# Cached-page attention as one stream beside projection and recurrence; projection by column blocks; values in four column groups; loops unrolled

## What is computed

```python
c, z, a, b, dq, dk, dv = split_proj(rmsnorm(x, w_norm_mix) @ w_in)      # 1024 -> 3592 columns
# prompt: gated DeltaNet, 4 heads, in chunks (state S carried from chunk to chunk)
g_out, conv_new, S = gdn_branch(c, z, a, b, ...)
# prompt: differential attention (two softmax maps a head)
# sample rows: differential attention over 8192 cached positions and the new one
k_past = cache_k[page_table].reshape(8, 8192, 4, 2, 64)
v_past = cache_v[page_table].reshape(8, 8192, 4, 128)
s = einsum('bqhcd,bkhcd->bhcqk', q, k) * 64 ** -0.5                     # past and new
p = softmax(s)
o = einsum('bhqk,bkhv->bqhv', p[:, :, 0] - lam * p[:, :, 1], v)
# output projection, residual, mixture of experts (32, two for a row), final norm
```

## Time and profile before

| | us |
|---|---|
| timed runs, median of three | 3375.11 |
| lowest and highest | 3366.74, 3377.62 |
| span of the profiled execution | 3370.8 |
| projection, to its last copy from PSUM | 0 to 491.9 |
| from there to the first tile's convolution | 491.9 to 535.1 |
| tile 0 (no values) | 535.1 to 706.9 |
| tiles 1 to 7 | 706.9 to 1826.1 |
| tile 8 (no keys) and the end of the phase | 1826.1 to 1934.2 |
| all other phases | 1934.2 to 3370.8 |

### The profile page before, as it was taken

How to read it: one execution, slowest core, us unless ns; L and a number is a source line. 1 busy time by engine, 2 the same in 40 slices (tenths; PEclk the granted TensorE clock), 3 DMA queues, 4 the chain that set the end, 5 groups by cost and what they waited for, 6 DMA issues and landing times. The chain is left out here.

```text
span 3370.8 us, 24571 instructions
## 1 busy us (share of the span) xinstructions
PE 2405.1 (71%) x7774; PEld 1179.5 (35%) x7774; DVE 1474.7 (44%) x2111; ACT 357.5 (11%) x661; POOL 991.5 (29%) x887
## 2 busy tenths in 40 slices
PE   8999981547565564748485738896991888988991
PEld 3444431413122222313131325554441434444440
DVE  1110106777777686868686254553332111111115
ACT  1000000000000000000000003332110111111111
POOL 0000004657575756657574200000002111111102
PEclk9999995669787887879797955687985989999996
DMA  6011015466565656566565342001211888888985
GB/s 229 35 56 42 36 55 199 146 240 221 222 250 218 254 214 249 218 227 230 212 252 191 112 156 93 10 7 43 75 62 41 292 297 280 305 282 280 310 297 187
DMA packets 213473, 600.37 MB, mean 178 GB/s; under 512 B 25619, under 2 KB 130915, under 8 KB 173078
## 3 DMA queue, kind: packets, MB, share of 16 engines
q0 software_dynamic: 57200, 351.91, 27.8%
q1 hardware_dynamic: 156161, 247.86, 21.7%
q10 hardware_dynamic: 64, 0.02, 0.0%
HBM read 537.07 MB, written 62.89 MB: 178 GB/s over the span
## 5 line engine op out<-in xcount | busy, mean ns | idle before, releaser
L820 PE MATMUL ps<-gd_vals,gd_w 128*4 128x512 f32 x1024 | 507.8, 636 | 344.7 <-DVE gd_w L795 278.7
L257 PE MATMUL ps<-pj_w_in,pj_xT 128*128 128x512 f32 (+1 forms) x1152 | 458.9, 559 | 10.6 <-ACT pj_xT L203 10.6
L1709 PE MATMUL ps<-ex_w_gu,ex_xT 128*128 128x512 f32 x768 | 384.2, 659 | 83.2 <-DMA ex_w_gu<-in_w_up 83.2
L688 DVE TENSOR_REDUCE gd_s<-gd_keys 128x32 f32<-128x2048 f32 x128 | 291.0, 2280 | 110.8 <-POOL gd_keys L444 109.4
L820 PEld LDWEIGHTS ps<-gd_vals,gd_w 128*4 128x4 f32 x1024 | 78.7, 89 | 665.6 <-issue 545.7
L257 PEld LDWEIGHTS ps<-pj_w_in,pj_xT 128*128 128x128 f32 x1152 | 211.5, 193 | 259.5 <-issue 258.0
L444 POOL TENSOR_TENSOR gd_keys<-gd_keys,gd_q 128x2048 f32<-128x2048 f32 x56 | 262.6, 4689 | 107.3 <-DMA gd_keys<-in_cache_k,gd_k_index 55.4
L1709 PEld LDWEIGHTS ps<-ex_w_gu,ex_xT 128*128 128x128 f32 x768 | 160.6, 212 | 302.5 <-issue 300.0
L680 DVE TENSOR_TENSOR gd_keys<-gd_keys,gd_q 128x2048 f32<-128x2048 f32 x72 | 261.9, 3637 | 0.0
L1681 DVE COPY ex_hhT<-ps 128x256 f32<-128x256 f32 x48 | 20.4, 424 | 432.8 <-PE ps L1722 432.8
L234 DVE COPY pj_proj<-ps 128x512 f32<-128x512 f32 (+1 forms) x36 | 20.2, 560 | 410.3 <-PE ps L257 410.3
(11 more groups left out here) (357 smaller groups left out, 3027.5 us busy)
## 6 DMA issues: line engine op xcount, KB each, us to landing
ex_w_gu<-in_w_gate SPq DMA_DIRECT2D x48, 1024.0 KB, 10.0
ex_w_gu<-in_w_up SPq DMA_DIRECT2D x48, 1024.0 KB, 12.3
ex_w_d<-in_w_down SPq DMA_DIRECT2D x48, 1024.0 KB, 7.1
gd_cs<-scr_proj SPq DMA_DIRECT2D x36, 768.0 KB
scr_ys<-ex_y POOLq DMA_DIRECT2D x48, 512.0 KB, 7.1
scr_proj<-pj_proj POOLq DMA_DIRECT2D x9, 1796.0 KB, 6.0
pj_w_in<-in_w_in SPq DMA_DIRECT2D x7, 2048.0 KB, 19.6
pj_x<-in_x SPq DMA_DIRECT2D x10, 512.0 KB, 3.3
```

The costliest lines, as they stand in the source:

```text
L257: last = pe.matmul(ps[:, 2 + n % 4, 0:w], xT[:, par, c * P:(c + 1) * P], w_in[:, c, o:o + w], start=(c == 0), stop=(c == KD - 1))
L688: v.tensor_reduce(s[:, CHUNK * i:CHUNK * (i + 1), :], keys[:, i % RING].rearrange("p a (c j) -> p a c j", j=DQ), AX_X, ALU.add).then_inc(k ...
L820: last = pe.matmul(ps[0:H, 0, :], w[:, g, :], vals[:, c % RING, j, :], start=(g == 0), stop=False)
L1709: last = pe.matmul(ps[:, GU_BANKS[par], :], xT[:, par, c * P:(c + 1) * P], w_gu[:, par, c, :], start=(c == 0), stop=(c == KD - 1))
```

## The change

The cached-page attention becomes a class `Decode` with a running number of the chunk on each engine, used by both phases. The 128 key chunks and 128 value chunks of the eight rows are one stream.

- **Projection by column blocks.** xT of all nine tiles stays in SBUF; w_in goes through two buffers of 512 columns. The order is a list of 72 units (block, tile). It begins with the q and k blocks of the last tile, which holds the sample rows, and ends with the eight gate columns, which now stay in SBUF (`dec.ab`). The x tiles lie at first in the buffers of the values and of q. ScalarE takes all units from PSUM (five banks), through four stages to stores on SP's queue.
- **The stream in the projection.** After the first two units the sample q and k are stored, loaded, rotated, stored, and q is loaded into all partitions. Then VectorE multiplies and reduces 64 key chunks. From unit 21 to 62 TensorE weighs one value chunk after each unit, 42 in all. POOL gathers both and does the all-reduces, in one order.
- **The stream in the recurrence.** A plan gives each of tiles 0 to 7 eight key chunks, one ahead of the levels and one in each level: the first, third, fifth and seventh of them multiplied on VectorE, the others on POOL. Value chunks go in halves of two matmuls to places around and in the levels, as far as their weights are ready: 16, 21, 11, 21, 11, 21, 11, 21, 21 halves in the nine tiles, and 18 halves are left behind the last tile.
- **Softmax lags the scores.** A batch's subtraction, sum and weights come at the fourth, fifth and seventh key of the next batch, with s and w held twice. Only the last batch has no next keys.
- **Values in four column groups.** The four pages of a chunk go to four column groups of the array and to partitions 0, 32, 64 and 96 of the bank; the four partial sums are stored apart and added at the end.
- The new token's score is computed in eight partitions in the projection. The loops over the tiles are unrolled, and POOL's index copies go, since a chunk's index column is now known.

```diff
+FIRST_WEIGH = 21
+BLOCKS = [C_DQ, C_DK, C_DV, 0, 512, 1024, C_Z, C_A]
+UNITS = [(0, LAST), (1, LAST)] + [(0, t) for t in range(LAST)] + [(1, t) for t in range(LAST)] + \
+        [(n, t) for n in range(2, 8) for t in [LAST, *range(LAST)]]
...
+    def reduce(self, n, on_pool=False):
+        dve, b, i = self.nc.vector, n // CHUNKS, n % CHUNKS
+        if b:
+            self.soften(b - 1, i)
...
+        dve.tensor_reduce(self.s[:, b % 2, CHUNK * i:CHUNK * (i + 1), :], self.keys[:, n % RING].rearrange("p a (c j) -> p a c j", j=DQ),
+                          AX_X, ALU.add).then_inc(self.k_used, 1)
...
+            last = pe.matmul(self.ps[32 * j:32 * j + H, 0, :], self.w[:, b % 2, g, :], self.vals[:, n % RING, j, :],
+                             start=(g == j), stop=(j > 0 and g == N_PAGES - CHUNK + j), tile_position=(0, 32 * j))
...
+                for n in range(RING):
+                    dec.gather_keys()
+                pool.wait_ge(xn_ready, TILES)
+                for n in range(RING):
+                    dec.gather_values()
+                for n in range(K_PROJECT):
+                    b, i = n // CHUNKS, n % CHUNKS
+                    dec.gather_keys()
+                    m = n - CHUNKS - T_W
+                    if i == CHUNKS - 1:
+                        dec.all_reduce_max(b)
+                    if b and i == T_EXP:
+                        dec.all_reduce_sum(b - 1)
+                    if m >= 0:
+                        dec.gather_values()
...
+                scales(5, 9)
+                for s in range(5, 9):
+                    normalize(s)
+                dve.wait_ge(dec.q_loaded, 16)
+                for n in range(K_PROJECT):
+                    if n % CHUNKS == 0:
+                        dec.new_token(n // CHUNKS)
+                    dec.multiply(n)
+                    dec.reduce(n)
...
+                for u in range(2, len(UNITS)):
+                    unit(u)
+                    if u - 2 + 3 < TILES:
+                        turn(u + 1)
+                    dec.weigh(CHUNK * weigh_in_project(u))
...
+                    refill(t, -1)
+                    for lev in range(7):
+                        product(t, lev)
+                        if lev == 1:
+                            pool.wait_ge(zt_ready, t + 1)
...
+                        if lev == 2:
+                            conv_tap(t + 1, 2)
...
+                        refill(t, lev)
...
                     for lev in range(7):
                         dve.wait_ge(p_ps, 7 * t + lev + 1)
                         v.tensor_tensor(prod[:], bank(7), bc(levels[:, lev:lev + 1, :], *HP), ALU.mult).then_inc(p_ready, 1)
-                        if with_k:
-                            score(t, lev + 3)
+                        scores(t, lev)
                         dve.wait_ge(dT_ps, 7 * t + lev + 1)
                         v.tensor_tensor(TT[:].rearrange("p a h j -> p a (h j)"), TT[:].rearrange("p a h j -> p a (h j)"), ps[:, 3:5, :], ALU.subtract).then_inc(t_ready, 1)
-                        if with_k and lev % 2 == 0:
-                            keys_times_query(t, lev + 4)
...
+                        if lev < 6:
+                            products(t, lev + 1)
```

More of the change, by code:

```diff
@@ L227, in _ @@
[L227 to L236 removed]
+                v = nc.vector
@@ L262, with unit @@
-CHUNK = 4
-CHUNKS = N_PAGES // CHUNK
-PRE_LOADS = 11 + CHUNK
-RING = 4
-def phase_recurrence_and_decode(nc, ps, A, keep):
+                def unit(u):
+                    n, t = UNITS[u]
+                    w = width(u)
+                    if u >= 5:
+                        pe.wait_ge(evac, u - 4)
+                    pe.wait_ge(w_loaded[n % 2], 16 * (n // 2 + 1))
+                    pe.wait_ge(xT_ready, order.index(t) + 1)
+                    for c in range(KD):
+                        last = pe.matmul(ps[:, 3 + u % 5, 0:w], xT[:, t, c * P:(c + 1) * P], w_in[:, n % 2, c, 0:w], start=(c == 0), stop=(c == KD - 1))
+                    last.then_inc(mm_done, 1)
@@ L510, in _, with product @@
+                def product(t, lev):
+                    n = plan.keys.get((t, lev))
+                    if n is not None and plan.on_pool(n):
+                        dec.multiply_on_pool(n)
+                for i in (2, 3, None):
+                    conv_tap(0, i)
+                for t in range(TILES):
                     ch.begin(t)
-                    products(1)
-                    refill_values(0, 1)
-                    products(3)
-                    refill_values(2, 3)
+                    refill(t, -2)
+                    product(t, -1)
@@ L690, in _, with products, scores @@
-                for t, with_k, with_v in turns(dve):
-                    base = D_STEPS * t
+                dve.wait_ge(gate_c, 1)
+                def products(t, lev):
+                    n = plan.keys.get((t, lev))
+                    if n is not None and not plan.on_pool(n):
+                        dec.multiply(n)
+                def scores(t, lev):
+                    n = plan.keys.get((t, lev))
+                    if n is not None:
+                        if n % CHUNKS == 0:
+                            dec.new_token(n // CHUNKS)
+                        dec.reduce(n, plan.on_pool(n))
@@ L827, in _, with weigh @@
-                for t, with_k, with_v in turns(pe):
-                    if with_v:
-                        weigh(t, 0, 2)
+                pe.wait_ge(c_loaded, 16 * C_LOADS)
+                def weigh(t, lev, first=True, last=True):
+                    n = plan.halves[t, lev]
+                    if not (first and last):
+                        n = (n + 1) // 2 if first else n // 2
+                    dec.weigh(n * CHUNK // 2)
+                for t in range(TILES):
+                    weigh(t, -2)
```

864 lines of the change are left out of this document (469 added, 395 removed).

## The result

The changed kernel takes 3035.45 us (median of four runs, 3032.37 to 3053.42) against 3376.36 before (a fourth run stands beside the three above); the ratio is 0.900, with a 95% interval of 0.898 to 0.903. So 341 us went; 290 were forecast. The profiled execution spans 3030.7 us.

What follows compares the result with a forecast made beforehand. TensorE alone was taken to bound the projection, a chain across engines the recurrence tiles. Projection to 586, tile 0 at 615, tiles to 1526, tail to 1644 against 1934: 290 saved, 3085 us forecast, range 2960 to 3210.

Steps and rivals of the forecast that it cites:

- The column price: Projection: a value chunk in four column groups costs TensorE 2.2 us, so 42 chunks cost 92 us.
- the narrow units: Projection: the narrow blocks of eight columns take some 1.7 us each, 15 us in all.
- Rival 1: Value chunks: all four column groups run at once, 0.86 us a chunk, 3025 us in total; chance 0.15.
- the estimate of 27 for the block: Projection start: the second column block, behind four x tiles and beside four key gathers, takes about 27 us to load.
- The 10 of waiting at unit 21: Projection: TensorE reaches unit 21 before the first softmax weights are ready and waits 10 us.
- The tile's own chain: Recurrence: 29 us to the decay matrices, 56 in seven levels, 17 behind them; 102 a tile.
- The sum's pauses: Recurrence, tiles 0, 2, 4, 6: the sum's all-reduce delays POOL's next product by 14 us each, 56 in all.
- The softening's 4.5 a batch: Recurrence: seven softmax operations add about 4.5 us for each of four batches, 18 in all.
- The last batch: End of the recurrence's keys: with no next keys to hide behind, its maximum to its weights costs 21 us.
- Rival 2: Value chunks: column groups do not overlap, 3.43 us a chunk, 52 more in the projection, 3144 in total; chance 0.18.
- Rival 3: Recurrence: TensorE idles between levels and runs at 1.2 GHz, 9 us more a tile, 3157 in total; chance 0.18.
- Rival 4: Projection: POOL's one gather queue starves it; losing 7.1 us more in each of 42 units undoes the gain; chance 0.04.

## Why the prediction came out as it did

The sign was right, the time lay in the range, and 290 of 341 us were found. By its own sum, against the changed kernel's stages:

| | predicted | measured | difference |
|---|---|---|---|
| projection ends | 586 | 558.2 | -27.8 |
| from there to tile 0 | 29 | 24.7 | -4.3 |
| tiles 0 to 7 | 911 | 884.6 | -26.4 |
| tile 8 to its last state | 76 | 75.4 | -0.6 |
| tail, outputs, to the next phase | 42 | 47.2 | +5.2 |
| the phases behind | 1436.6 | 1440.6 | +4.0 |
| span | 3080.6 | 3030.7 | -49.9 |

**The column price was mis-sized.** "If TensorE starts instructions in order ... 5 steps of 0.43 instead of 8", so 2.2 a chunk: it was 1.16, near the lower bound of 0.86. From unit 2 (55.1) to the narrow units (532.1) are 477 us; less 61 x 6.87 and 7 for turns, 42 chunks took 51 instead of 92. The records and the kernel with two groups show that this working fails: every group goes on with its own next instruction while the others work. Rival 1 had the mechanism. The Trainium skill's page "TensorEngine Tiling (Array Packing)", Overview, was right with its up to 4x inside a chunk (two steps instead of eight). Where the shape changes, instructions begin 0.52 to 0.53 us apart instead of 0.43 (393.14 to 393.67, 394.12 to 394.64, 200.94 to 201.47), which makes the 0.3 around each chunk; that fits the drain of its Tiling Modes, but no run here separates it from other costs of the change.

**Three terms of the projection erred the other way or fell out.** Unit 2 started at 55.1 and not at 43: four gathers beside the second column block cost more than the estimate of 27 for the block allowed (unit 1 began at 37.3); with the gathers moved it started at 43.9. The narrow units took 26.1 instead of 15, for whose 1.7 each no row stood: the first three take 1.8 to 1.9 us, the other six 3.2 to 3.4, and the granted clock is 0.60 in that stretch (1.2 GHz from the fourth on). The 10 of waiting at unit 21 did not appear: the weights were ready at 198.99, and TensorE came to them at 199.97. Together -41 + 12 + 11 - 10 = -28.

**The tile's own chain was right.** Odd tiles: 28 to the decay matrices (predicted 29), 56.5 in the levels (56), 16 behind them (17), 100.5 against 102. That the pair of VectorE and POOL sets a level's time was shown by taking POOL out: 47.4.

**The sum's pauses were right in place and size**: 14 each predicted, 16 measured, and taking them away made even and odd tiles equal. The softening's 4.5 a batch were counted beside them; the 16 hold what it costs, 2 to 3 by the kernel with the sum on TensorE. The last batch cost 7 (107.2 against 100.5), not 21: its second all-reduce follows the first directly and no product waits behind them. Tile 0 is longer by 10 at its start, where two of VectorE's own tap operations take 5.0 and 4.9 us instead of 1.76 beside POOL's, and it then waits 3.4 for POOL's last; no step had that. Together -12 + 8 - 18 - 14 + 10 = -26.

**The rivals.** Rival 2's price was nearly right: against four groups 42 x (3.43 - 1.16) = 95 us by it, 106 measured, since the 0.3 around a chunk comes on top of the 3.43; and, as it had it, the tiles do not change.

Rival 3 came half true: the clock is 0.67 to 0.69 in even tiles and 0.75 to 0.81 in odd ones, not far above the 0.59 that it named, but what could be seen of it is up to 3 us a tile and not 9. In the levels of an odd tile it is not on the path: with one group TensorE had 10 us more to do there, at a clock of 0.91 instead of 0.84, and the levels took 57.0 instead of 56.5 (tile 3), since the chain runs through VectorE and POOL; for the levels of the even tiles no run shows it. Behind the levels the chain is TensorE's and ScalarE's. From the last subtraction to the new state, in tile 5 and in tile 6 of the changed kernel:

```profile
1228.80:1239.30 10.50, 9.44 (x52) 8.73 (x56) 0.06 (x1) 1.20 (x2) 1.58 (x2) 0.61 0.33 112
1346.40:1353.80 7.40, 6.14 (x52) 5.64 (x56) 0.06 (x1) 1.20 (x2) 1.92 (x3) 1.00 0.74 256
```

The forecast had put 2 us for this into its 17 behind the levels. With all products on VectorE the stretch ran at 1.00 in tiles 0 to 6 and took 7.4, a part of that kernel's gain.

Rival 4 fell: units keep their 8.03 us spacing to the end, TensorE is busy 526 of 558 us, and the DMAs move 285 GB/s. (Its 7.1 us a unit should have been 290 / 42 = 6.9.) That the forecast held 290 of 341 in spite of several wrong terms is partly luck: errors of opposite sign met in the projection.

**Left open.** The experts phase is 725 to 741 us in every kernel with the change and 717.8 in the one trace of before, with the same code. No run here tells why. No run undoes the unrolled loops or the new order of the units by itself, so their shares, put at nothing for the loops, are not shown.

## What to carry to other kernels

Work moved beneath a stage that one engine fills costs that engine's own extra instructions and little else: here 1.1 us for a pair of chunks that cost 5.2 where all engines are chained. Before splitting a product between VectorE and POOL, count POOL's pauses around all-reduces and who stands behind them; the split was slower than VectorE alone. And two edits that each remove a wait need not add up, since the first wait may have kept a later collision apart.

## What the runs showed of the hardware

- Value matmuls in different column groups overlap fully: 3.7, 2.0 and 1.16 us for a chunk in one, two and four groups, of which some 0.3 lies where the shape changes.
- A VectorE operation with two operands in SBUF waits for POOL's running tensor operation: 0.69 became 7.91 (behind two in a row), 2.28 became 5.6, 1.76 became 5.0. It works the other way too: in tile 0, where the two engines took turns, POOL's taps lasted 4.8 to 5.0 instead of 3.42. Reductions, and operations that read PSUM, kept their time (2.27 and 0.69). The Trainium skill's "SBUF — State Buffer", Who interferes with whom, states this lock for two SBUF inputs against a POOL operation that reads SBUF; the trace agrees.
- POOL's indirect gathers were held up too: of 61 that began during one of VectorE's key products in the changed kernel, 60 ended 0.8 to 1.1 us behind the product, and the median was 2.7 us; 21 beside a reduction took 0.94.
- A POOL all-reduce between tensor operations came after a pause of 5.7 to 9.1 us, and the next tensor operation after another of 7 to 9; a gather right behind the all-reduce started at once (802.56). A second all-reduce soon behind the first took only its 0.41 us (1447.47 in tile 7). In the projection, where POOL does nothing but gathers between its all-reduces, only the first had a pause (8.2 us).
- The 52 matmul instructions and two copies from a tile's last subtraction to its new state took 7.4 us at a granted clock of 1.00 and 10.5 at 0.61.
